# Third attention of a three-layer kernel: the squares of q and k summed over the partitions by two fp32r passes with a matrix of ones

## What is computed

```python
q, k, v, g_sb, x_lru, g_lru = jnp.split(proj, ...)
qh = rmsnorm_2(heads(q), q_norm_gain[l])   # y = x * rsqrt(mean(x * x) + EPS) * gain, per head
kh = rmsnorm_2(heads(k), k_norm_gain[l])
z = jnp.einsum('bqhd,bkhd->bhqk', qh, kh) * scale
log_fail = jnp.where(mask, jax.nn.log_sigmoid(-z), 0.0)
after = lax.cumsum(log_fail, axis=3, reverse=True) - log_fail
w = jnp.where(mask, jnp.exp(jax.nn.log_sigmoid(z) + after), 0.0)
out = jnp.einsum('bhqk,bkhd->bqhd', w, v)
```

## Time and profile before

| | |
|---|---|
| time, median of 3 runs | 2234.86 us (2234.73 to 2235.54) |
| the profiled execution's own time | 2232.39 us |
| its span, first to last instruction | 2230.6 us |
| mean granted clock of TensorE, share of full | 0.994 |
| stage `stick`, eight heads | from about 1476 to 2010 us of the span |

### The profile page before, as it was taken

One profiled execution on the slowest core, in us unless ns is written; L12 is line 12 of the kernel. 1 busy time (PEld: TensorE's weight loads), 2 busy tenths in 40 slices (PEclk: granted clock), 3 DMA queues, 4 the chain that ended last, 5 costly groups with the idle time before them and its releaser, 6 DMA issues.

```text
span 2230.6 us, 31366 instructions
## 1 busy us (share of the span) xinstructions
PE 2186.6 (98%) x10276; PEld 1811.0 (81%) x10276; DVE 1456.5 (65%) x2593; ACT 962.8 (43%) x1861; POOL 159.8 (7%) x202
## 2 busy tenths in 40 slices
PE   7999999999899999999999999999999999998999
PEld 5778888888788888888888788888888888886887
DVE  6567777777542568888888833576767676767432
ACT  5444444444432525555554533535453544355221
POOL 1100000000201010000000121300000000002000
PEclk9999999999999999999999999999999999999999
DMA  6322222223624622322222453442333233325552
GB/s 195 106 58 80 80 80 80 80 80 109 200 76 113 182 76 85 84 82 81 81 81 82 150 174 90 155 121 76 103 89 99 82 105 87 102 79 156 171 140 66
DMA packets 371279, 234.97 MB, mean 105 GB/s; under 512 B 4900, under 2 KB 345124, under 8 KB 371238
## 3 DMA queue, kind: packets, MB, share of 16 engines
q1 hardware_dynamic: 371238, 234.46, 36.6%
HBM read 210.06 MB, written 24.38 MB: 105 GB/s over the span
## 4 chain that ended last, share of the span: by engine, by line
PE 94%; DVE 3%; DMA 1%; ACT 1%; SPq 0%; issue 0%; POOL 0%; POOLq 0%; DVEq 0%; ACTq 0%
PE pp L577 26%; PE pp L579 26%; PE pp L578 26%; DMA xT<-x 1%; PE ps L577 1%; PE ps L599 1%; PE ps L579 1%; PE ps L578 1%; PE ps L601 1%; PE ps L600 1%; PE pt L1038 1%; DVE w_lo L552 1%; PE po L601 1%; PE po L599 1%; PE po L600 1%; PE po L1668 1%
## 5 line engine op out<-in xcount | busy, mean ns | idle before, releaser
L577 PE MATMUL pp<-act_hi,w_hi 128*128 128x512 f32 x2432 | 972.6, 400 | 28.5 <-DVE act_lo L796 13.3
L579 PE MATMUL pp<-act_hi,w_lo 128*128 128x512 f32 x2432 | 953.5, 392 | 0.0
L578 PE MATMUL pp<-act_lo,w_hi 128*128 128x512 f32 x2432 | 952.4, 392 | 0.0
L552 DVE TENSOR_TENSOR w_lo<-raw,w_hi 128x512 fp32r<-128x512 f32 x676 | 459.5, 707 | 331.4 <-ACT w_hi L543 328.7
L577 PEld LDWEIGHTS pp<-act_hi,w_hi 128*128 128x128 f32 x2432 | 460.0, 189 | 130.1 <-issue 25.7
L543 ACT ACTIVATE w_hi<-raw 128x512 fp32r<-128x512 f32 (+1 forms) x692 | 404.5, 620 | 356.0 <-PE pp L579 212.3
L579 PEld LDWEIGHTS pp<-act_hi,w_lo 128*128 128x128 f32 x2432 | 459.2, 189 | 98.8
L578 PEld LDWEIGHTS pp<-act_lo,w_hi 128*128 128x128 f32 x2432 | 460.3, 189 | 92.8 <-issue 4.1
L1726 ACT ACTIVATE s_prob<-ps,s_minus,s_q_scale 128x256 f32<-128x256 f32 x128 | 71.0, 559 | 143.2 <-DVE s_minus L1801 143.2
L1271 POOL TENSOR_TENSOR act_lo<-y_whole,act_hi 128x512 fp32r<-128x512 f32 x20 | 28.6, 1461 | 1038.6 <-ACT act_hi L1265 1038.6
L1105 ACT ACTIVATE prob<-ps,minus,q_scale 128x512 f32<-128x512 f32 (+1 forms) x64 | 39.0, 615 | 96.9 <-DVE minus L1167 96.9
(11 more groups left out here) (358 smaller groups left out, 2664.3 us busy)
## 6 DMA issues: line engine op xcount, KB each, us to landing
raw<-w_in SPq DMA_DIRECT2D x48, 1024.0 KB, 5.9
raw<-swa_w_in SPq DMA_DIRECT2D x36, 1024.0 KB, 5.6
raw<-mla_w_in SPq DMA_DIRECT2D x23, 1024.0 KB, 5.8
raw<-mla_w_out SPq DMA_DIRECT2D x16, 1024.0 KB, 7.0
raw<-swa_w_out SPq DMA_DIRECT2D x16, 1024.0 KB, 6.4
raw<-w_out SPq DMA_DIRECT2D x16, 1024.0 KB, 7.8
y_whole<-y_feature_major SPq DMA_DIRECT2D x9, 1024.0 KB, 7.3
raw<-mla_w_ukv SPq DMA_DIRECT2D x16, 512.0 KB, 4.4
```

Source lines behind the costliest of these rows:

```text
L552: q.eng.tensor_tensor(dst, raw_piece(tile, p), high, ALU.subtract).then_inc(s_lo, 1)
L577: q.eng.matmul(psum[:, :], wh, ah, start=start and n == 0, stop=False)
L578: q.eng.matmul(psum[:, :], wh, al, start=False, stop=False)
L579: last = q.eng.matmul(psum[:, :], wl, ah, start=False, stop=stop and n == PIECE // P - 1)
```

## The change

In the third attention the square of q (and of k) is split after it is computed: ScalarE copies it to an fp32r high part, VectorE subtracts for the low part, and TensorE sums both with a matrix of ones that is fp32r as well, by two matmuls into one PSUM group. The ones are copied once, in the norm ahead of the stage. The two parts go to buffers that the recurrence input's split uses earlier in the same body (`d_xc_hi`, `d_xc_lo`). The one square buffer and the two part buffers serve q, k and the next head in turn, hence the waits that are added. The core of the diff:

```diff
+            d_ones = sb("d_ones", [P, P], F32R, scope)
+            d_sq_hi, d_sq_lo = d_xc_hi, d_xc_lo
...
+            copy_hi(q, d_ones[:, :], c("ones"), "ones")
...  stick_T
-            q.eng.wait_ge(*q.at("A.q_sq"))
+            q.eng.wait_ge(*q.at("V.q_sq_lo"))
             if attn:
                 q.eng.wait_ge(*q.at("V.pt_lo0"))
-            q.eng.matmul(pt[0][:, :], c("ones"), d_sq, start=True, stop=True).then_inc(*q.did("q_norm"))
+            q.eng.matmul(pt[0][:, :], d_ones[:, :], d_sq_hi[:, :], start=True, stop=False)
+            q.eng.matmul(pt[0][:, :], d_ones[:, :], d_sq_lo[:, :], start=False, stop=True).then_inc(*q.did("q_norm"))
...
-            q.eng.wait_ge(*q.at("A.k_sq"))
-            q.eng.matmul(pt[1][:, :], c("ones"), d_sq, start=True, stop=True).then_inc(*q.did("k_norm"))
+            q.eng.wait_ge(*q.at("V.k_sq_lo"))
+            q.eng.matmul(pt[1][:, :], d_ones[:, :], d_sq_hi[:, :], start=True, stop=False)
+            q.eng.matmul(pt[1][:, :], d_ones[:, :], d_sq_lo[:, :], start=False, stop=True).then_inc(*q.did("k_norm"))
...  stick_A
                 q.eng.wait_ge(*q.at("V.q_ev"))
+                if attn:
+                    q.eng.wait_ge(*q.at("V.k_sq_lo", i - 1))
                 q.eng.activation(d_sq, d_q[:, :], ACT.Square).then_inc(*q.did("q_sq"))
+                q.eng.wait_ge(*q.at("A.q_sq"))
+                if attn:
+                    q.eng.wait_ge(*q.at("T.k_norm", i - 1))
+                copy_hi(q, d_sq_hi[:, :], d_sq, "q_sq_hi")
...
                 q.eng.wait_ge(*q.at("V.k_ev"))
+                q.eng.wait_ge(*q.at("V.q_sq_lo"))
+                q.eng.activation(d_sq, d_k[:, :], ACT.Square).then_inc(*q.did("k_sq"))
+                q.eng.wait_ge(*q.at("A.k_sq"))
                 q.eng.wait_ge(*q.at("T.q_norm"))
-                q.eng.activation(d_sq, d_k[:, :], ACT.Square).then_inc(*q.did("k_sq"))
+                copy_hi(q, d_sq_hi[:, :], d_sq, "k_sq_hi")
             hi_(GS, 2, 3)
...  stick_V
                 q.eng.tensor_tensor(d_q[:, :], pp[0][:, :], rstd[:, :], ALU.mult).then_inc(*q.did("q_ev"))
+                q.eng.wait_ge(*q.at("A.q_sq_hi"))
+                if attn:
+                    q.eng.wait_ge(*q.at("T.k_norm", i - 1))
+                sub_lo(q, d_sq_lo[:, :], d_sq, d_sq_hi[:, :], "q_sq_lo")
...
             lo_(GS, 2, 3)
             if proj:
+                q.eng.wait_ge(*q.at("A.k_sq_hi"))
+                q.eng.wait_ge(*q.at("T.q_norm"))
+                sub_lo(q, d_sq_lo[:, :], d_sq, d_sq_hi[:, :], "k_sq_lo")
                 multiplied(q, Tile("stick", i, V3))
                 q.eng.tensor_tensor(d_v[:, :], pp[0][:, :], rstd[:, :], ALU.mult).then_inc(*q.did("v_ev"))
```

More of the change, by code:

```diff
@@ L145 @@
         "A": ("hi0 hi1 hi2 hi3 hi4 hi5 hi6 hi7 hi8 hi9 hi10 hi11 sq0 sq_f0 hi12 hi13 hi14 hi15 sq1 sq_f1 root "
-              "root_b abs exp").split(),
+              "root_b ones abs exp").split(),
         "V": ("gains lo0 lo1 lo2 lo3 lo4 lo5 lo6 lo7 lo8 lo9 lo10 lo11 x0 x1 lo12 lo13 lo14 lo15 rstd mean_a mean_b "
@@ L154 @@
         "A": ("tanh_s abs3 exp3 abs2 exp2 abs1 exp1 abs0 exp0 ln3 ln2 ln1 ln0 weights3 weights2 weights1 weights0 "
-              "xc_hi w_hi pt_hi3 pt_hi2 pt_hi1 pt_hi0 tanh_l tanh_r tanh_i q_sq a tanh_a m q_root q_hi k_sq k_root "
-              "k_hi v_hi").split(),
+              "xc_hi w_hi pt_hi3 pt_hi2 pt_hi1 pt_hi0 tanh_l tanh_r tanh_i q_sq q_sq_hi a tanh_a m q_root q_hi k_sq "
+              "k_sq_hi k_root k_hi v_hi").split(),
         "V": ("gate silu_s sp3 seen3 after3 log_w3 masked3 sp2 seen2 after2 log_w2 masked2 sp1 seen1 after1 log_w1 "
               "masked1 sp0 seen0 after0 log_w0 masked0 xl_ev conv0 conv1 conv2 conv3 xc_lo w_lo pt_lo3 pt_lo2 "
-              "pt_lo1 pt_lo0 gl_ev silu_l log_a q_ev y a2 m2 ix u h y_lru q_rms qn q_lo k_ev v_ev k_rms kn k_lo "
-              "v_lo").split(),
+              "pt_lo1 pt_lo0 gl_ev silu_l log_a q_ev q_sq_lo y a2 m2 ix u h y_lru q_rms qn q_lo k_ev k_sq_lo v_ev "
+              "k_rms kn k_lo v_lo").split(),
     },
```

## The result

Over 22 runs of each, the changed kernel takes 2237.71 us (median; 2236.29 to 2241.51) and the kernel before 2233.89 (2229.53 to 2235.88). The ratio is 1.0020, with a 95% interval of 1.0014 to 1.0027: slower by 4.5 us, 3.1 to 6.0 (the two medians lie 3.8 apart). The forecast was +6.3, to 2241.2, with 2237 to 2245 as its own range. Both intervals lie above no change.

A forecast was written before the change was run, and what follows sets the result against it. TensorE, with a matmul always in flight, bounds the stage. Head 0 gives -0.80 us, heads 1 to 7 give 7 x (1.82 - 0.80) = +7.1, together +6.3 on 2234.86: 2241.2, own range 2237 to 2245.

The forecast's parts named there:

- The sum's price: TensorE's sum over partitions: 0.86 us as fp32, 0.46 as two fp32r passes, a gain of 0.40 per sum, 16 sums.
- The key's stall: TensorE waits for k_sq_lo at the key's sum, 1.82 us in each of heads 1 to 7, bounds 1.5 to 2.1.
- The query's gain: The 0.40 us saved at the query's sum brings TensorE to the key's sum earlier, at 1796.82 instead of 1797.22.
- TensorE has no other idle time in these heads: In the heads with the stall, nothing gives the 1.82 us back.
- Per head and sum: Heads 75.2 us apart instead of 74.2; head 0 -0.80, heads 1 to 7 together +7.1, in all +6.3 us.
- The time: Whole kernel, as a median of timed runs: 2234.86 + 6.3 = 2241.2 us.
- where the low clock falls: In the last stage, the place of TensorE's low clock can move the time by 1.7 us either way.
- No stall: Rival: k_sq_lo is ready in time at the key's sum in every head, gain 6.4 us, 2228.4; chance 8%.
- The clock: Rival: granted clock falls after each of the seven stalls at the key's sum, +18.2 us, 2253.1; chance 11%.
- Dear passes: Rival: two fp32r passes cost what the fp32 matmul costs, stall 1.42 us per head, +9.9, 2244.8; chance 9%.
- Cover: The ones' copy and the query's split cost nothing in idle time; v_ev and k_lo, queued later, make nothing late.

The follow-up runs named there:

- e3: Changed kernel with k_sq_lo moved ahead of the low parts of GS pieces 2 and 3 on VectorE; 73.80 us per head, ratio 0.9986 to the kernel before.
- e5: e3 with V3 piece 2's low part ahead of q_rms and k_ev ahead of GS pieces 0 and 1; 73.23 us per head, ratio 0.9960 to kernel before.
- e1: Changed kernel with only the query's sum as two fp32r passes, the key's one fp32 matmul; 74.22 us per head, one run 2234.61 us beside 2234.05.
- e6: Changed kernel with v_ev put ahead of k_sq_lo on VectorE; 75.80 us per head, ratio 1.0052 to the kernel before.
- e4: e3 with the low part of V3 piece 2 moved ahead of q_rms on VectorE; 73.64 us per head, one run 2226.64 us beside 2232.92.

## Why the prediction was right

- **The sum's price.** Forecast 0.86 down to 0.46. The trace shows 0.45, and e3 and e5 show 0.42 to 0.43 per sum in the distance of the heads. Right.
- **The key's stall.** Forecast: k_sq_lo 18.33 us behind y's start. Measured 18.33. The two GS pieces in front of it were the reason, as e3 shows by moving k_sq_lo ahead of them. That the figure is exact is luck in part, as two errors of 0.08 us cancel: k_sq was put down as unchanged and started 14.58 us behind y instead of 14.50, and k_sq_hi was given 0.12 us behind k_sq for its two waits and took 0.04. The handover to TensorE was 0.16 us for 0.17.
- **The query's gain.** This is the step that failed: "TensorE would have been there at 1797.22 - 0.40 (the query's gain) = 1796.82". It was there at 17.09 us behind y's start, which is 1797.23 on that scale. The 0.40 had been lost at V3 piece 2 (e1). So "TensorE has no other idle time in these heads" was wrong as well: 0.12 us per head was lost at that piece before the change. The matmuls' busy time (534 of 534 us) and the matmuls' waits hide it; the starts show it, and so does the wait of the weight loads. The same total came out because the end of the stall is set by k_sq_lo alone: 0.43 at V3 piece 2 and 1.40 at the key's sum make the 1.82 that I put in one place.
- **Per head and sum.** Forecast 75.2 us from head to head, measured 75.20. For the stage: head 0 gains 0.83 against 0.80 (from its query's sum to its key's it takes 14.08 us instead of 14.50, and from the query's sum to the transposes of v 20.00 instead of 20.84, with no wait; k_sq_lo was done 0.1 us ahead of the sum's weight load, as forecast), heads 1 to 7 lose 0.98 each: +6.0 against a forecast of +6.3.
- **The time.** +4.5 (3.1 to 6.0) and +6.0 (4.0 to 8.0). The profiles show about 3 us less in the last stage (62.2 on average before, 60.1 and 60.2 after, with one stall's 1 us in it), the timed runs up to 1.5. The forecast had 1.7 either way for "where the low clock falls" there. The traces show the low clock as the larger part of it, worth up to about 3.3 us in a profile, but the forecast had no way to tell which way it would go. In the absolute time, 2237.71 for 2241.2, another 1.0 us is the starting point: 2234.86 was the median of three runs, 2233.89 is that of 22.
- **The rivals.** No stall: out, seven waits. It was also priced wrong: with the stall away and no other edit the gain is 3.8 us in the stage (e3), not 6.4. The clock: out for this size of wait, since it stayed at 1.00 with waits of 1.1 and, in e6, of 1.7 us (idle between records); the rule of "TensorE: Matmul & The Clock Gate", section "A second HAM failure mode: psum-queue depth-cycling", in the Trainium skill on kernels that idle between groups did not come to bear here. Dear passes: out.
- **Cover.** The query's split, the copy of the ones, v_ev and k_lo made nothing late, as forecast: TensorE's waits are the two named.

## What to carry to other kernels

An instruction that a critical engine starts to wait for costs the engine's whole in-order queue in front of it, not its own length: here two instructions of under 0.7 us each, with two pieces queued between them, cost a stall of 1.40 us, and moving one of them ahead of the pieces took it away. Before counting a saving on the critical engine, follow it to the next operand it needs: if that is made by an engine whose order runs from an earlier event, the saving dies there. Look for such places in the starts of the instructions and in the waits of the weight loads, since a loss of 0.1 us shows in no wait of the matmuls here; then move the producer first and make the work cheaper second.

## What was not expected of the hardware

A short wait of TensorE does not show as idle time of its matmuls: at V3 piece 2 of the kernel before, the record of the late matmul is 0.50 us instead of 0.39 and no idle time is listed, though two intervals take 0.57 us instead of 0.45. Its weight load does have the wait, 0.27 us for `w_lo`. And the stretch between the last two y moved by up to 4.4 us (59.3 to 63.7) between kernels that differ only in the heads ahead of it. It was short where the low clock came for 3.5 us (7 in e4) and long where it came for 10; these runs do not show what decides between them.
